# A transformer block pair on one core: the output projection and the next up projection in token halves

## The reference, cut to what matters

```python
x = x + g1 * rms_norm(y_lat, mix_post_g[i])                  # y_lat = attention output @ w_o
ffn = (ffn_w_up[i], ffn_w_dw[i], ffn_b_dw[i], ffn_w_down[i])
f_lat = conv_ffn(modulate(rms_norm(x, ffn_pre_g[i]), sh2, sc2), *ffn)

def rms_norm(x, g):
    y = x * lax.rsqrt(jnp.mean(x * x, axis=-1, keepdims=True) + RMS_EPS)
    return y * g

def conv_ffn(h, w_up, w_dw, b_dw, w_down):
    gate, val = jnp.split(h @ w_up, 2, axis=-1)
    gate = depthwise_conv(gate, w_dw) + b_dw                 # width 3, along the tokens
    return (jax.nn.gelu(gate) * val) @ w_down
```

## Time and profile before

| what | before |
|---|---|
| time, median of 3 runs | 1708.3 us (1707.18 to 1716.6) |
| the profiled execution | 1706.25 us, of which the traced span is 1704.4 us |
| PE busy | 1604.5 us (94%), 9293 matmuls |
| POOL, DVE, ACT busy | 820.0, 735.5, 733.1 us |
| chain that ended last, by engine | PE 80%, DVE 7%, issue 5%, POOL 3%, DMA 3%, ACT 2% |
| granted PE clock, mean | 0.98 of full speed |

### The profile page before, as it was taken

One profiled execution on the slowest core, in us unless ns is written; L12 is line 12 of the kernel. 1 busy time (PEld: TensorE's weight loads), 2 busy tenths in 40 slices (PEclk: granted clock), 3 DMA queues, 4 the chain that ended last, 5 costly groups with the idle time before them and its releaser, 6 DMA issues.

```text
span 1704.4 us, 25340 instructions
## 1 busy us (share of the span) xinstructions
PE 1604.5 (94%) x9293; PEld 1282.8 (75%) x9293; DVE 735.5 (43%) x1384; ACT 733.1 (43%) x1093; POOL 820.0 (48%) x444
## 2 busy tenths in 40 slices
PE   4889999999999999999999999999996999999996
PEld 1666565769998988888888787777775788888885
DVE  1564796664447544434442623544432433333002
ACT  1531242545674555454322424454553544443221
POOL 0454334567888844444555643343425344444553
PEclk9899999999999999999999999999997999999998
DMA  8767787355565522233575321212102233233321
GB/s 305 256 191 218 209 233 225 134 186 160 177 188 150 169 95 91 95 98 95 231 276 187 95 87 44 63 32 63 44 26 87 62 98 97 89 97 97 97 79 49
DMA packets 71651, 224.82 MB, mean 132 GB/s; under 512 B 8080, under 2 KB 15760, under 8 KB 71312
## 3 DMA queue, kind: packets, MB, share of 16 engines
q1 hardware_dynamic: 68832, 215.72, 40.6%
q10 hardware_dynamic: 2736, 7.95, 1.3%
HBM read 218.13 MB, written 5.51 MB: 131 GB/s over the span
## 4 chain that ended last, share of the span: by engine, by line
PE 80%; DVE 7%; issue 5%; POOL 3%; DMA 3%; ACT 2%; DVEq 0%; ACTq 0%; POOLq 0%; SPq 0%
PE bank L1633 21%; PE bank L1635 20%; PE bank L1634 20%; PE bank L1603 2%; POOL bias L738 2%; PE bank L1955 2%; PE bank L1577 1%; DVE bank L1300 1%; PE bank L1957 1%; PE bank L1956 1%; DVE x_lat L1207 1%; PE bank L1796 1%; PE bank L2028 1%; DMA ada_raw<-in_mod_w 1%; PE bank L2038 1%
## 5 line engine op out<-in xcount | busy, mean ns | idle before, releaser
L642 POOL TENSOR_TENSOR w_lo<-w_raw,w_hi 128x1024 fp32r<-128x1024 f32 (+1 forms) x288 | 684.8, 2384 | 727.8 <-ACT w_hi L800 727.8
L800 ACT ACTIVATE w_hi<-w_raw 128x1024 fp32r<-128x1024 f32 (+1 forms) x288 | 298.4, 1037 | 237.3 <-PE bank L1635 187.0
L1633 PE MATMUL bank<-h_hi_lat,w_hi 128*128 128x512 f32 x856 | 339.6, 397 | 0.6 <-DVE u_lat L1324 0.6
L1635 PE MATMUL bank<-h_hi_lat,w_lo 128*128 128x512 f32 x856 | 335.6, 392 | 0.0
L1634 PE MATMUL bank<-h_lo_lat,w_hi 128*128 128x512 f32 x856 | 332.9, 389 | 0.0
L1633 PEld LDWEIGHTS bank<-h_hi_lat,w_hi 128*128 128x128 f32 x856 | 160.9, 188 | 46.7 <-issue 11.6
L1635 PEld LDWEIGHTS bank<-h_hi_lat,w_lo 128*128 128x128 f32 x856 | 160.7, 188 | 37.1
L1634 PEld LDWEIGHTS bank<-h_lo_lat,w_hi 128*128 128x128 f32 x856 | 160.7, 188 | 35.0
L1633 PE MATMUL bank<-h_hi_ctx,w_hi 128*128 128x256 f32 x544 | 157.5, 290 | 12.4 <-DVE h_lo_ctx L1231 8.1
L1635 PE MATMUL bank<-h_hi_ctx,w_lo 128*128 128x256 f32 x544 | 154.0, 283 | 0.0
L1634 PE MATMUL bank<-h_lo_ctx,w_hi 128*128 128x256 f32 x544 | 153.9, 283 | 0.0
(11 more groups left out here) (218 smaller groups left out, 2698.0 us busy)
## 6 DMA issues: line engine op xcount, KB each, us to landing
w_raw<-in_ffn_w_up SPq DMA_DIRECT2D x132, 512.0 KB, 3.5
ada_raw<-in_mod_w SPq DMA_DIRECT2D x52, 512.0 KB, 5.8
w_raw<-in_cv_w_pw SPq DMA_DIRECT2D x48, 512.0 KB, 5.7
w_raw<-in_ffn_w_down SPq DMA_DIRECT2D x48, 448.0 KB, 3.3
mod_rows<-in_mod_rows SPq DMA_DIRECT2D x32, 512.0 KB, 5.6
w_raw<-in_ffn_w_down SPq DMA_DIRECT2D x24, 512.0 KB, 3.5
shifted_lat<-u_lat SPq DMA_DIRECT2D x32, 270.0 KB, 6.6
w_raw<-in_na_w_qk SPq DMA_DIRECT2D x16, 512.0 KB, 4.0
```

Source lines behind the costliest of these rows:

```text
L642: pool.tensor_tensor(wlo[s][:, 0:kt * P], raw[s][:, 0:kt * P], whi[s][:, 0:kt * P].bitcast(F32), ALU.subtract).then_inc(w_lo, 1)
L800: act.activation(whi[s][:, 0:kt * P], raw[s][:, 0:kt * P], ACT.Copy).then_inc(w_hi, 1)
L1633: pe.matmul(b, whi[s][:, w], hi[:, a], start=(first and k == 0), stop=False)
L1635: ins = pe.matmul(b, wlo[s][:, w], hi[:, a], start=False, stop=(last and k == kts - 1))
```

## The change

Iteration 1 of phase `o` and iteration 0 of `up1` are made in two halves of 256 tokens. For `o`, PE makes the four tiles for the first 256 tokens, then the four for the last 256. The chain between the phases has its own semaphores (`al_...`) and runs once for each half, with 256-wide operations, a root and a reciprocal on 64 partitions, and its own bank for the spread reciprocal (6 and 7). For `up1`, each half is made as: all products of tiles 0, 1 and 2 with `h_hi_lat`, then theirs with `h_lo_lat`, then tile 3. POOL takes the additions to x of the odd tiles of the second half. The order on the engines is written out anew:

```diff
+            def o_halves(ph, base):                       # POOL
+                for j in range(4):
+                    pool.wait_ge(o_half_ev, j + 1)
+                    add_half(0, j)
+                for j in range(4):
+                    pool.wait_ge(evac, ph.evac0 + 4 + j + 1)
+                    add_half(1, j)
+                    lo_ahead(ph, 1, j, True)
+                for k in range(1, KD, 2):
+                    tile = half_of(k, 1)
+                    pool.wait_ge(al_y, KD + k + 1)
+                    pool.tensor_tensor(X[LAT][:, tile], X[LAT][:, tile], al.Y[:, tile], ALU.add).then_inc(al_x_odd, 1)
...
+            def o_halves(ph, q0, hi_ahead):               # ACT
+                for j in range(4):
+                    act.wait_ge(o_half, j + 1)
+                    half_out(0, j).then_inc(o_half_ev, 1)
+                al_root(0, 1)
+                out_b(0)
+                hi_ahead(ph, 1, 0, True)
+                al_squares(0, 0, 2)
+                out_b(1)
+                hi_ahead(ph, 1, 1, True)
+                al_squares(0, 2, 5)
+                out_b(2)
+                hi_ahead(ph, 1, 2, True)
+                al_squares(0, 5, 8)
+                al_root(0, 2)
+                out_b(3)
+                al_hi_h(0, 0, 2)
+                al_root(1, 1)
+                al_hi_h(0, 2, 4)
+                hi_ahead(ph, 1, 3, True)
+                al_hi_h(0, 4, 8)
+                al_squares(1, 0, 8)
+                al_root(1, 2)
+                al_hi_h(1, 0, 8)
...
-            post_now(al)                                  # DVE
-            pre_now(al)
+            al_recip(0, 1)
+            al_update(0)
+            al_recip(0, 2)
+            al_scale(0)
+            al_recip(1, 1)
+            al_low(0)
+            al_update(1)
+            al_recip(1, 2)
+            al_scale(1)
+            al_low(1)
             up_phase("up1", 1, sum0["down1"])
...
+            def o_by_halves(ph):                          # PE
+                for j in range(4):
+                    split_wait(ph, 1, j)
+                    pe.wait_ge(evac, ph.evac0 + j + 1)
+                    half_products(bank[j], ph.slot(j), Ohi, Olo, 0, 0, KD).then_inc(o_half, 1)
+                between_parts = {0: (6, lambda: al_sum(0)), 1: (3, lambda: al_inverse(0, 1))}
+                for j in range(4):
+                    pe.wait_ge(o_half_ev, j + 1)
+                    k = 0
+                    if j in between_parts:
+                        k, step = between_parts[j]
+                        half_products(bank[j], ph.slot(j), Ohi, Olo, 1, 0, k)
+                        step()
+                    half_products(bank[j], ph.slot(j), Ohi, Olo, 1, k, KD).then_inc(blk, 1)
+                al_sum_squares(0)
+                al_sum(1)
+                al_inverse(0, 2)
+
+            def up_by_halves(ph):
+                hi, lo = Hhi[LAT], Hlo[LAT]
+                for h in range(2):
+                    if h:
+                        al_sum_squares(1)
+                        al_inverse(1, 2)
+                    else:
+                        split_wait(ph, 0, 2)
+                        pe.wait_ge(evac, ph.evac0)
+                    for k in range(KD):
+                        pe.wait_ge(al_hi, h * KD + k + 1)
+                        for j in range(3):
+                            for part in (whi[j], wlo[j]):
+                                pe.matmul(bank[j][:, half_of(0, h)], part[:, k * P:(k + 1) * P], hi[:, half_of(k, h)],
+                                          start=(part is whi[j] and k == 0), stop=False)
+                        if k == KD - 2 and h == 0:
+                            al_inverse(1, 1)
+                    for k in range(KD):
+                        pe.wait_ge(al_lo, h * KD + k + 1)
+                        for j in range(3):
+                            ins = pe.matmul(bank[j][:, half_of(0, h)], whi[j][:, k * P:(k + 1) * P],
+                                            lo[:, half_of(k, h)], start=False, stop=(k == KD - 1))
+                            if h and k == KD - 1:
+                                ins.then_inc(blk, 1)
+                    if h == 0:
+                        split_wait(ph, 0, 3)
+                    ins = half_products(bank[3], 3, hi, lo, h, 0, KD)
+                ins.then_inc(blk, 1)
```

More of the change, by code:

```diff
@@ L275, in build @@
         SCORES = [bank[5], bank[6]]
+        RINV_OF = [bank[6], bank[7]]
         TURNED = [bank[7], bank[3]]
@@ L696, in body @@
                     tiles = 0
+                    if name == "o" and last:
+                        o_halves(ph, base)
+                        return
                     for j in range(ph.per):
@@ L773, in _ @@
             up_phase("up1", "o")
-            y_phase("down1", "up1", chains["att_l"].stat0 + 1)
+            y_phase("down1", "up1", 4)
             fin = chains["out_l"]
@@ L840, in hi_h, with al_root, al_squares @@
                                ACT.Identity, bias=mod[:, ds(t * 2 + (ch.pre[1] + j), 1)]).then_inc(h_hi, 1)
+            def al_root(h, stage):
+                act.wait_ge(al_stat, 2 * h + stage)
+                act.activation(root_t[half_rows(h), :], STAT[half_rows(h), 0:P], ACT.Sqrt, bias=RMS_EPS,
+                               scale=1.0 / D).then_inc(al_rms, 1)
+            def al_squares(h, k0, k1):
+                for k in range(k0, k1):
+                    if h and k % 2:
+                        act.wait_ge(al_x_odd, k // 2 + 1)
+                    else:
+                        act.wait_ge(al_x, KD + k // 2 + 1 if h else k + 1)
+                    act.activation(SQ[LAT][:, half_of(k, h)], X[LAT][:, half_of(k, h)], ACT.Square).then_inc(al_sq, 1)
@@ new lines, in al_hi_h, with half_out, out_b @@
+            def al_hi_h(h, k0, k1):
+                for k in range(k0, k1):
+                    act.wait_ge(al_t, h * KD + k + 1)
+                    act.activation(Hhi[LAT][:, half_of(k, h)], SQ[LAT][:, half_of(k, h)], ACT.Identity,
+                                   bias=mod[:, al.pre[1] + k:al.pre[1] + k + 1]).then_inc(al_hi, 1)
+            def o_halves(ph, q0, hi_ahead):
+                def half_out(h, j):
+                    act.wait_ge(summed, q0 + 4 + 4 * h + j)
+                    part = half_of(0, h)
+                    act.activation(al.Y[:, half_of(4 + j, h)], bank[j][:, part], ACT.Copy)
+                    return act.activation(sq[j % 2][:, part], bank[j][:, part], ACT.Square)
+                def out_b(j):
+                    act.wait_ge(blk, ph.blk0 + 4 + j + 1)
+                    half_out(1, j).then_inc(evac, 1)
+                for j in range(4):
[21 more added lines that the diff above has]
+                al_hi_h(1, 0, 8)
@@ L924, in body @@
                     tiles = 0
+                    if name == "o" and last:
+                        o_halves(ph, q0, hi_ahead)
+                        return
                     for j in range(ph.per):
@@ L1688, in o_begun, with al_sum, al_sum_squares @@
                 return ins
+            def al_sum(h):
+                pe.wait_ge(summed, sum0["o"] + KD + 1 + 4 * h)
+                for g in (2 * h, 2 * h + 1):
+                    ins = pe.matmul(STAT[BLK32 * g:BLK32 * (g + 1), 0:P], ones[:, 0:BLK32],
+                                    acc[LAT][:, g * P:(g + 1) * P], start=True, stop=True)
+                ins.then_inc(al_stat, 1)
+            def al_sum_squares(h):
+                for k in range(KD):
+                    pe.wait_ge(al_sq, h * KD + k + 1)
+                    for g in (2 * h, 2 * h + 1):
+                        ins = pe.matmul(STAT[BLK32 * g:BLK32 * (g + 1), 0:P], ones[:, 0:BLK32],
+                                        SQ[LAT][:, k * L + g * P:k * L + (g + 1) * P],
+                                        start=(k == 0), stop=(k == KD - 1))
+                ins.then_inc(al_stat, 1)
@@ new lines, in al_inverse @@
+            def al_inverse(h, stage):
+                pe.wait_ge(al_rcp, 2 * h + stage)
+                for g in (2 * h, 2 * h + 1):
+                    pick = ident[half_rows(h), BLK32 * g:BLK32 * g + 1]
+                    pick = bass.AP(tensor=pick.tensor, offset=pick.offset, ap=[list(pick.ap[0]), [0, P]])
+                    ins = pe.matmul(RINV_OF[h][:, g * P:(g + 1) * P], pick, inv_t[half_rows(h), :],
+                                    start=True, stop=True)
+                ins.then_inc(al_spread, 1)
@@ new lines, in half_products @@
+            def half_products(b, s, hi, lo, h, k0, k1):
+                for k in range(k0, k1):
+                    w, a = slice(k * P, (k + 1) * P), half_of(k, h)
+                    out = b[:, half_of(0, h)]
+                    pe.matmul(out, whi[s][:, w], hi[:, a], start=(k == 0), stop=False)
+                    pe.matmul(out, whi[s][:, w], lo[:, a], start=False, stop=False)
+                    ins = pe.matmul(out, wlo[s][:, w], hi[:, a], start=False, stop=(k == KD - 1))
+                return ins
@@ L1696, in body @@
```

(14 more changed lines are left out.)

81 lines of the change are left out of this document (52 added, 29 removed).

## The result

| what | before | after |
|---|---|---|
| time, median | 1705.67 us (12 runs, 1702.0 to 1716.6) | 1712.2 us (12 runs, 1707.16 to 1724.11) |
| ratio to before | | 1.0036, interval 1.002 to 1.0053 |
| the profiled execution, span | 1706.25, 1704.4 us | 1710.23, 1708.4 us |

A forecast was written before the change was run, and what follows sets the result against it. PE bounds the kernel, busy 94%, so only its waits around the norm count: -10.7 + 4.5 + 1.4 + 1.4 + 6.4 + 0.7 + 0.6 = +4.3 us on the middle 1707.2, giving 1711.5 us; range 1703 to 1718.

The forecast's parts named there:

- x7 ready: Last x tile of the first half's update on DVE, held by POOL's block 2: 1306.2 instead of 1299.3.
- wait for bank 0: Before iteration 1 of `up1`: banks 0 to 2 finish together, leaving 2.8 us cover for 9.2; 6.4 us new waiting.
- low clock behind it: Iteration 1 of `up1` starts at the low clock again after the bank 0 wait: +1.4 us.
- The price of narrow matmuls: 256-wide matmuls on PE come 0.118 us apart at full clock: +0.7 us each for `o` and `up1`.
- The rival of the weight loads: Narrow matmuls on PE bound by twice as many weight loads: +12 us, 1719 or more; chance 0.03.
- the +21 us: Estimate from the skill page's issue gaps, 98 ns per 256-column matmul on PE: halving costs some +21 us.
- The start: First `up1` matmul on PE at 1311.8, 10.7 us earlier than before.
- the rival of the light holds: DVE slips between POOL's steps, `up1` starts near 1306: 1704 to 1706 us; chance 0.22.
- The hold of 1.6 behind block 3: Between the halves of `up1`, DVE is held 1.6 us behind POOL's block 3.
- The wait between the halves: PE, free after the first half of `up1`, waits 4.5 us for DVE's chain; second half starts at 1329.6.
- The rival of the slower chain: Second half's DVE and POOL chain binds, starting it at 1334 or later: +9 to +14, 1716 to 1721; chance 0.14.
- The rival that bank 0 is no bound: Before iteration 1, 6.4 + 1.4 us fall away: -3.5, 1704; with light holds 1696 to 1698; chance 0.06 for both.

The follow-up runs named there:

- again: The changed kernel run once more, unaltered, for a second trace: ratio to before 1.0026 (1.001 to 1.0042).
- no_port: Changed kernel with the first half's eight DVE additions to x reading a PSUM bank instead of y (wrong sum); one run, mark to iteration 1 67.52 us against 71.71.

## Why the prediction was right

Its steps in before's clock (0.24 added to the first trace, 1.84 taken from the second):

| step | forecast | after | again |
|---|---|---|---|
| wait for the last block of `o` | 0.6 | 0.60 | 0.49 |
| PE comes to the sum of squares | 1300.3 | 1301.05 | 1300.98 |
| x7 ready | 1306.2 | 1303.59 | 1303.53 |
| `up1` starts | 1311.8 | 1308.79 | 1308.73 |
| first half done | 1325.1 | 1323.63 | 1322.36 |
| second half starts | 1329.6 | 1328.75 | 1327.48 |
| wait for bank 0 | 6.4 | 6.21 | 6.20 |
| iteration 1 starts | 1348.8 | 1347.99 | 1346.78 |
| low clock behind it | 1.4 | 2.2 | 2.8 |
| sum | +4.3 | +4.2 | +3.6 |

**The price of narrow matmuls** held: (1281.36 - 1276.04) / 47 = 0.113 us in the first halves of `o`, 0.118 further on. The rival of the weight loads is gone, and so is the +21 us by the figures of the Trainium skill, TensorE: Matmul & The Clock Gate, section Back-to-back issue gap.

**The start** is the term that was mis-sized: -13.7 instead of -10.7. The step that failed is "block 2 runs from 1303.4 to 1305.8, and x7 is ready at 1306.2". The holds are there, as `no_port` shows, but DVE's last two additions ran from 1302.07 to 1303.35, and POOL began block 2 at 1303.04, when they were nearly done: it ran when the forecast said, but x7 didn't have to wait for it. What they met was POOL's short addition to the sum, of 0.96 us, and the first 0.3 us of block 2. The forecast had 6.9 us of holds, the trace has 7.15 - 4 x 0.75 = 4.15 for the four pairs. The truth lies between the forecast and the rival of the light holds. The start is also less bound to x7 than the forecast had it: in `no_port` x was whole 4.15 us earlier and the start came 1.8 earlier. The hold of 1.6 behind block 3 came as priced: DVE's eight low parts of the first half took 4.88 us beside it and 3.25 alone in the second half.

**Two errors the other way** made up for it. The first half of `up1` lasted 14.8 us and not 13.3, since PE was slow for 6.1 us and not 3.0; in the second trace it lasted 13.6, near the forecast. And the slow start of iteration 1 cost 2.2 and 2.8 us, and not the 1.4 priced. The wait between the halves (from the end of the first to the start of the second) was 5.12 in both traces, forecast 4.5: the chain over DVE was sized to half a microsecond. The rival of the slower chain, with a start at 1334 or later, did not happen.

**Bank 0** was right in mechanism and in size, and the experiments confirm the cause: with tiles 0 and 1 first the wait is 2.66, with the table loads out of the chain 3.65, with both and an earlier start none. The rival that bank 0 is no bound did not happen.

So the total was right to 0.1 us in the first trace partly by luck: a start 3.0 us better against 2.3 us more of low clock and 0.6 of waiting. The 1711.5 us, beside 1712.2 measured, are luck in part too. They were counted from 1707.2, and the median of the kernel before over 12 runs is 1705.67; by the ratio the change costs 6.1 us (4.4 in the repeat), by the traces some 4.

## What to carry to other kernels

Cutting a phase into halves hides one half's chain behind the other's products, but ask who consumes the tiles: what used to be finished in turn is finished at once at the end, and the next iteration waits for the first bank. Finish the tiles whose consumers' chain is longest first, and move what can be done ahead (a table load, a weight's low part) out of it, even where it cost nothing before. Here these repairs turned +0.3% into -0.4%. The halves themselves brought nothing before the repairs.

## What the runs showed of the hardware

The low clock's length behind a pause is not a property of the kernel. Behind the first pause of the same kernel PE stayed slow for 6.1 us in one trace and 2.9 in the other; in the kernel before 3.1, and with an edit that adds no wait 5.3. In `no_port` there was no slow matmul behind that pause at all. Over the other traces and pauses without filler in which the clock fell, PE stayed slow for 2.9 to 6.1 us. The moment of the fall moves too: in three kernels with the same work up to there it came before the last spread of the first half, in the changed kernel after it. A single trace can thus not price a fall better than to some 3 us of slow matmuls, which is 1.5 us of time.

The holds between DVE and POOL, in contrast, repeat: the four pairs of additions took 2.22, 0.75, 2.90 and 1.28 us in the one trace and 2.25, 0.75, 2.88 and 1.28 in the other. They hang on which instruction of POOL a pair meets: with POOL's low parts moved behind them all four took 0.76, and with one input in a bank 0.75.
